# Seven products instead of eight for each pair of chunks in two down projections

## The reference

```python
h = rms_norm(x, ffn_norm_g[l])                       # first block
g = jnp.einsum('bld,df->blf', h, w_gate[l])
u = jnp.einsum('bld,df->blf', h, w_up[l])
x = x + jnp.einsum('blf,fd->bld', jax.nn.silu(g) * u, w_down[l])
...
n2 = rms_norm_2(h, norm_mlp_pre[l])                  # second block
hid = jnp.square(jax.nn.relu(jnp.einsum('bsd,df->bsf', n2, w_up[l])))
mlp_out = jnp.einsum('bsf,fd->bsd', hid, w_down[l])
h = h + rms_norm_2(mlp_out, norm_mlp_post[l])
```

## Time and profile before

| | |
|---|---|
| median of three runs | 758.38 us |
| the profiled execution | 758.59 us |
| its span, first to last instruction | 757.3 us (1.3 us less) |
| TensorE clock granted | 0.999 of full speed |
| PE matmul busy | 739.8 us, 98% |
| PE weight load busy | 641.1 us, 85% |
| DVE busy | 457.8 us, 60% |
| ACT busy | 373.3 us, 49% |
| POOL busy | 112.5 us, 15% |
| DMA | 130.46 MB, mean 172 GB/s |

### The profile page before, as it was taken

One profiled execution on the slowest core, in us unless ns is written; L12 is line 12 of the kernel. 1 busy time (PEld: TensorE's weight loads), 2 busy tenths in 40 slices (PEclk: granted clock), 3 DMA queues, 4 the chain that ended last, 5 costly groups with the idle time before them and its releaser, 6 DMA issues.

```text
span 757.3 us, 11043 instructions
## 1 busy us (share of the span) xinstructions
PE 739.8 (98%) x4394; PEld 641.1 (85%) x4394; DVE 457.8 (60%) x635; ACT 373.3 (49%) x535; POOL 112.5 (15%) x138
## 2 busy tenths in 40 slices
PE   6999999999999999999999999999999999999996
PEld 5877778999999999888888888888779899998895
DVE  5898695766555555465747555674948754455433
ACT  6666754644444434285443534664338644444431
POOL 2867550100000000001110000000302111001110
PEclk9999999999999999999999999999999999999999
DMA  9642142787665666446536543474535766656511
GB/s 318 207 132 82 58 160 92 229 284 220 189 212 172 195 216 208 133 142 219 169 110 195 194 139 112 123 250 147 178 107 198 260 192 187 206 184 191 180 46 56
DMA packets 70179, 130.46 MB, mean 172 GB/s; under 512 B 5312, under 2 KB 29072, under 8 KB 70128
## 3 DMA queue, kind: packets, MB, share of 16 engines
q1 hardware_dynamic: 68144, 125.00, 52.3%
q0 software_dynamic: 1552, 4.20, 1.7%
q10 hardware_dynamic: 432, 0.56, 0.2%
HBM read 128.62 MB, written 1.05 MB: 171 GB/s over the span
## 4 chain that ended last, share of the span: by engine, by line
PE 93%; DVE 3%; DMA 2%; issue 1%; ACT 1%; SPq 0%; DVEq 0%; ACTq 0%
PE psum L453 41%; PE psum L888 29%; PE psum L506 12%; PE psum L930 2%; DMA w_raw<-in_w_in 2%; PE psum L680 1%; PE psum L601 1%; PE psum L546 1%; PE psum L631 1%; PE psum L1058 1%; PE psum L582 1%; PE psum L652 1%; DVE b_ratio L2154 0%; PE psum L992 0%; PE psum L1020 0%
## 5 line engine op out<-in xcount | busy, mean ns | idle before, releaser
L1908 DVE TENSOR_TENSOR w_lo<-w_raw,w_hi 128x1024 fp32r<-128x1024 f32 x225 | 275.2, 1235 | 158.3 <-ACT w_hi L1284 157.7
L1284 ACT ACTIVATE w_hi<-w_raw 128x1024 fp32r<-128x1024 f32 x231 | 241.2, 1059 | 180.7 <-PE psum L888 78.6
L888 PE MATMUL psum<-h_hi,w_hi 128*128 128x256 f32 x608 | 170.3, 284 | 0.6 <-issue 0.6
L888 PE MATMUL psum<-h_hi,w_lo 128*128 128x256 f32 x608 | 169.5, 283 | 0.0
L888 PE MATMUL psum<-h_lo,w_hi 128*128 128x256 f32 x608 | 161.8, 281 | 0.0
L888 PEld LDWEIGHTS psum<-h_hi,w_hi 128*128 128x128 f32 x608 | 114.7, 189 | 1.7 <-issue 0.7
L888 PEld LDWEIGHTS psum<-h_hi,w_lo 128*128 128x128 f32 x608 | 114.4, 188 | 0.0
L888 PEld LDWEIGHTS psum<-h_lo,w_hi 128*128 128x128 f32 x608 | 111.1, 189 | 0.7
L453 PE MATMUL psum<-w_hi,h_hi 128*128 128x512 f32 (+1 forms) x240 | 94.5, 394 | 0.0
L453 PE MATMUL psum<-w_hi,h_lo 128*128 128x512 f32 (+1 forms) x240 | 93.0, 387 | 0.0
L453 PE MATMUL psum<-w_lo,h_hi 128*128 128x512 f32 (+1 forms) x240 | 92.9, 387 | 0.0
(11 more groups left out here) (303 smaller groups left out, 992.7 us busy)
## 6 DMA issues: line engine op xcount, KB each, us to landing
w_raw<-in_w_in SPq DMA_DIRECT2D x77, 512.0 KB, 4.5
w_raw<-in_w_down SPq DMA_DIRECT2D x54, 512.0 KB, 4.3
w_raw<-in_w_up SPq DMA_DIRECT2D x32, 512.0 KB, 4.4
w_raw<-in_w_gate SPq DMA_DIRECT2D x44, 256.0 KB, 2.9
w_raw<-in_w_up SPq DMA_DIRECT2D x44, 256.0 KB, 3.4
w_raw<-in_w_out SPq DMA_DIRECT2D x16, 512.0 KB, 4.0
w_raw<-in_w_branch_a SPq DMA_DIRECT2D x4, 512.0 KB, 4.6
w_raw<-in_w_branch_b SPq DMA_DIRECT2D x4, 512.0 KB, 4.6
```

The source lines that it names most:

```text
L888: mm = pe.matmul(outs, x[:, cols], y[:, kc, :], start=kc == 0 and n == 0, stop=kc == KC - 1 and n == (1 if i == 0 else 2))
L1284: act.activation(T.w_hi[:, k % SLOTS, :], T.w_raw[:, k % RAW_SLOTS, :], ACT.Copy).then_inc(S.w_rounded, 1)
L1908: dve.tensor_tensor(T.w_lo[:, k % SLOTS, :], T.w_raw[:, k % RAW_SLOTS, :], T.w_hi[:, k % SLOTS, :], ALU.subtract).then_inc(S.w_cut, 1)
```

## The change

The chunks of a down projection are taken in pairs (11 in the first, 16 in the second). The pair's product is a 2 x 2 block product: hidden values in four quarters (2 chunks x 2 token tiles), weights in four quarters (2 chunks x 2 output halves). Except in the last pair of each block it is formed with seven products of sums of quarters, where there were eight plain ones (Winograd's form of Strassen's method). `PRODUCT` gives each product's hidden quantity, weight quantity and PSUM bank; each is three matmuls of 512 columns.

- **Weight quarters.** POOL's queue brings them: `load_pair` the first three (768 KB), `load_twice` the fourth, written twice (512 KB), and `add_pair`, which adds the first two quarters, read from where they landed in SBUF, onto the two copies (an accumulating DMA, 512 KB, SBUF to SBUF). DVE forms two more sums (`sum_pair`, `sum_pair_rest`). ACT rounds and DVE cuts seven quantities, in parts of 3, 2 and 2 (`round_pair`, `cut_pair`). The arrays are laid out on the host so that each partition's data are contiguous.
- **Hidden quarters.** ACT first copies the up product out of PSUM (`take_up`, `take_hidden`). DVE forms four more quantities (`sum_hidden`, `_2`, `_3`), seven of 128 columns are rounded and cut. The second block's squares move from POOL to ACT.
- **PSUM.** The seven products hold banks 0 to 6 through the whole block; up has bank 7 alone, so each two up chunks wait until ACT has copied the two before.
- **Slots.** In the feed-forward parts fills have four slots; the other four hold every second pair's seven quantities.
- **End of a block.** The last but one pair ends products 1, 6, 7 and 5, from which ACT and DVE form what is added to each output quarter; the last pair is computed plainly into the banks of products 4, 2 and 3 and into bank 7 (`down_quarters`).

The diff, cut to its core:

```diff
+PRODUCT = {1: (1, 0, 2), 2: (3, 2, 0), 3: (7, 1, 5), 4: (2, 6, 6), 5: (5, 3, 1), 6: (6, 5, 3), 7: (4, 4, 4)}
+EARLY, LATE, MIXED, OWN = (1, 2, 3), (7, 5, 6, 4), (1, 6, 7, 5), (4, 2, 3)
+NEEDS = {1: 1, 2: 1, 3: 1, 7: 2, 5: 2, 6: 3, 4: 3}
+QUARTERS = {1: ((0, 0, 6), (1, 0, 0), (1, 1, 5), (0, 1, 7)), 2: ((0, 0, 6), (0, 1, 7), (1, 0, 0), (1, 1, 5))}
...
+    def down(q, products, first=False, last=False):
+        buf, i = pair_place(q)
+        pe.wait_ge(S.hidden_cut, q + 1)
+        for n_product, p in enumerate(products):
+            x, y, b = PRODUCT[p]
+            pe.wait_ge(S.pair_cut, pair_parts(q) + NEEDS[p])
+            x_hi, x_lo = T.hid_hi[:, i, x - 1, :], T.hid_lo[:, i, x - 1, :]
+            y_hi, y_lo = T.pair_hi[buf][:, y, :], T.pair_lo[buf][:, y, :]
+            for n, (u, v) in enumerate(((x_hi, y_hi), (x_hi, y_lo), (x_lo, y_hi))):
+                mm = pe.matmul(bank[b][:], u, v, start=first and n == 0, stop=last and n == 2)
...
+    up_first("up1", CUT["h2"], NORM["h2"], True, turn_x_right)
+    up_two(W.first["up1", 2], 3)
+    pe.wait_ge(S.up_taken, 2)
+    up_two(W.first["up1", 3], 7)
+    up_two(W.first["up1", 4], 6)
+    for i in range(2, PAIRS1):
...
+            pe.wait_ge(S.up_taken, 2 * i)
+            up_two(W.first["up1", 2 * i], 7)
+        down(i - 2, EARLY, first=i == 2)
+        pe.wait_ge(S.up_taken, 4 if i == 2 else 2 * i + 1)
+        up_two(W.first["up1", 2 * i + 1], 7)
...
+        down(i - 2, LATE, first=i == 2)
+    down(LAST1 - 1, MIXED, last=True)
+    down(LAST1 - 1, OWN)
+    down_quarters(1, QUARTERS[1][:3])
+    turn_pairs(T.x, (0, 1), (4, 6), [[(S.x_added, 9)], [(S.x_added, 10)]])
+    down_quarters(1, QUARTERS[1][3:])
...
+    pe.wait_ge(S.mixed_read, 1)
     product_piece("z", 1, 0)
+    turn_pairs(T.x, (2, 3), (2, 3), [[(S.x_added, 12)], ()])
     product_piece("z", 1, 1)
...
+    up_first("up2", CUT["h4"], NORM["h4"], False)
+    up_two(W.first["up2", 4], 3)
+    for i in range(2, PAIRS2):
+        if i > 2:
+            pe.wait_ge(S.up_taken, 2 * PAIRS1 + i)
+            up_two(W.first["up2", 2 * i], 7)
...
+        down(FIRST2 + i - 2, EARLY, first=i == 2)
...
+        down(FIRST2 + i - 2, LATE, first=i == 2)
+    down(LAST2 - 1, MIXED, last=True)
+    down(LAST2 - 1, OWN)
+    down_quarters(2, QUARTERS[2])
...
+            round_pair(q, 0)
+            round_hidden(q)
+            round_pair(q, 1)
+            if k < len(W.fills):
+                round_fill(k)
+            round_pair(q, 2)
+            if i > 2:
+                take_hidden(i)
+                square_hidden(i)
+            if k < len(W.fills):
+                round_fill(k + 1)
...
+            sum_hidden(q, 2 * PAIRS1 + i)
+            sum_hidden_2(q)
+            sum_hidden_3(q)
+            cut_pair(q, 0)
+            sum_pair(q)
+            cut_hidden(q)
+            sum_pair_rest(q)
+            cut_pair(q, 1)
+            if k < len(W.fills):
+                cut_fill(k)
+            cut_pair(q, 2)
+            if k < len(W.fills):
+                cut_fill(k + 1)
...
     post_out(0)
     add_out2(0)
-    cut_fill(W.first["up2", 0] + 0)
+    cut_fill(W.first["up2", 0] + 2)
     post_out(1)
     add_out2(1)
...
+    def load_twice(q):
...
+        elif q not in (1, FIRST2 + 1):
+            pool.wait_ge(S.pair_cut, pair_parts(q - 2) + 2)
+        pool.dma_start(T.pair_t[:, i, 0:n, :], W.pairs[q][:, 3:4, :].broadcast_to([P, n, WIDE])).then_inc(S.twice_landed[i], 16)
+    def load_pair(q):
...
+        elif q not in (0, FIRST2):
+            pool.wait_ge(S.pair_cut, pair_parts(q - 1))
+        pool.dma_start(T.pair_raw[i], W.pairs[q][:, 0:3, :]).then_inc(S.pair_landed[i], 16)
+    def add_pair(q):
+        i = pair_place(q)[1]
+        pool.wait_ge(S.twice_landed[i], pair_loads(q))
+        pool.wait_ge(S.pair_landed[i], pair_loads(q))
+        pool.dma_start(T.pair_t[:, i], T.pair_raw[i][:, 0:2, :], accum_op=ALU.add).then_inc(S.pair_added[i], 16)
...
+    pool.wait_ge(S.w_used, W.first["o", 1])
+    load_twice(FIRST2)
+    load_pair(FIRST2)
+    load_twice(FIRST2 + 1)
+    add_pair(FIRST2)
     for t in range(TILES):
         pool.wait_ge(S.post_mean, t + 1)
         root(T.stat[:, 4 + 2 * t:5 + 2 * t]).then_inc(S.post_root, 1)
     pool.wait_ge(S.x_mean, 4)
     root(T.row_scale[:, 3, :]).then_inc(S.x_root, 1)
+    load_pair(FIRST2 + 1)
+    add_pair(FIRST2 + 1)
+    for q in range(FIRST2 + 2, LAST2 + 1):
+        load_twice(q)
+        load_pair(q)
+        if q < LAST2:
+            add_pair(q)
```

More of the change, by code:

```diff
@@ L198, in used @@
     def used(self, name):
[L200 to L201 removed]
+        return self.first[name] + {"kva": 2}.get(name, 4)
 SEMAPHORES = """
@@ new lines, in up_two @@
+    def up_two(k, b):
+        for j in range(2):
+            up_group(k + j, bank[b][:, j * SEQ:(j + 1) * SEQ])
+    def down(q, products, first=False, last=False):
[8 more added lines that the diff above has]
+                mm = pe.matmul(bank[b][:], u, v, start=first and n == 0, stop=last and n == 2)
+            if last:
+                mm.then_inc(S.product_done, 1)
+        if products == LATE:
+            mm.then_inc(S.pair_used, 1)
@@ new lines, in down_quarters @@
+    def down_quarters(block, some):
+        q = (LAST1, LAST2)[block - 1]
+        buf, i = pair_place(q)
+        pe.wait_ge(S.hidden_cut, q + 1)
+        pe.wait_ge(S.pair_cut, pair_parts(q) + 2)
+        for t, half, b in some:
+            if b == 7:
+                pe.wait_ge(S.up_taken, 2 * PAIRS1 if block == 1 else 2 * PAIRS1 + PAIRS2)
+            for c in range(2):
+                y = ((0, 3), (2, 1))[c][half]
+                x_hi, x_lo = T.hid_hi[:, i, 2 * c + t, :], T.hid_lo[:, i, 2 * c + t, :]
+                y_hi, y_lo = T.pair_hi[buf][:, y, :], T.pair_lo[buf][:, y, :]
+                for n, (u, v) in enumerate(((x_hi, y_hi), (x_hi, y_lo), (x_lo, y_hi))):
+                    mm = pe.matmul(bank[b][:], u, v, start=b == 7 and c == 0 and n == 0, stop=c == 1 and n == 2)
+            mm.then_inc(S.quarter_done, 1)
@@ new lines, in copy_first @@
+    def copy_first(block):
+        act.wait_ge(S.pair_cut, pair_parts((LAST1, LAST2)[block - 1]))
+        act.wait_ge(S.product_done, len(MIXED) * (block - 1) + 1)
+        act.activation(T.form[block][0], bank[2][:], ACT.Copy).then_inc(S.first_copied, 1)
+    f = W.first["up1", 0]
+    round_to(f + 6)
+    take_up(0)
+    take_up(1)
+    round_fill(f + 6)
+    silu(0)
+    round_fill(f + 7)
+    silu(1)
+    for i in range(1, PAIRS1):
+        round_pair(i - 1, 0)
+        take_up(2 * i)
+        round_fill(f + 4 * i + 4)
+        silu(2 * i)
+        round_fill(f + 4 * i + 5)
+        round_hidden(i - 1)
+        round_pair(i - 1, 1)
+        round_pair(i - 1, 2)
+        take_up(2 * i + 1)
+        round_fill(f + 4 * i + 6)
+        silu(2 * i + 1)
+        if i < LAST1:
+            round_fill(f + 4 * i + 7)
@@ L1886, in scalar_program @@
+    copy_first(2)
+    for n, (t, half, _) in enumerate(QUARTERS[2]):
+        square_last(n, t, half, T.last[t, half])
     act.wait_ge(S.x_posted, 8)
@@ new lines, in vector_program, with end_last, scale_last @@
+    scale = [T.row_scale[:, 3, t:t + 1] for t in range(TILES)]
+    def end_last(n):
+        t, half, b = QUARTERS[2][n]
+        dve.wait_ge(S.quarter_done, 4 + n + 1)
+        own()
+        dve.tensor_tensor(T.last[t, half], bank[b][:], T.last[t, half], ALU.add).then_inc(S.formed, 1)
+    def scale_last(n):
+        t, half, _ = QUARTERS[2][n]
+        cols = slice(half * WIDE, (half + 1) * WIDE)
+        dve.wait_ge(S.formed, n + 1)
+        u = dve.scalar_tensor_tensor(T.tmp[:, t, cols], T.last[t, half], scale[t], T.bg[1][:, cols], ALU.mult, ALU.mult)
+        if half == 1:
+            u.then_inc(S.post_scaled, 1)
```

650 lines of the change are left out of this document (420 added, 230 removed).

## The result

The changed kernel took **783.27 us** (median of 4 runs, 778.5 to 784.06), the kernel before on the same chip 758.61 (4 runs, 758.03 to 759.13): ratio **1.031**, 95% interval 1.0289 to 1.0331. Forecast were 752.3 us and a range of 746 to 763. The forecast was wrong in sign, and the time lies outside its range. One execution of experiment 3 (770.64 us) is left aside for its lower mean granted clock, 0.91 where its other execution had 0.987.

A forecast was written before the change was run, and what follows sets the result against it. PE, busy 98% of the span, was taken as the bound. Span: 757.3 - 17.5 - 0.5 + 2.0 + 4.1 + 1.9 + 3.6 + 0.2 = 751.1 us; with 1.3 outside 752.4, stated as 752.3, 8-in-10 range 746 to 763.

The forecast's parts named there:

- some 7.5 us from the first issue, 7.0 from its own: Landing time of a pair's 768 KB load with 512 KB ahead of it in its queue.
- the circle of the second block: Load 7.0, sum 5.5, DVE and issue 7.0: 19.5 us against 21.2 over two steps; PE waits if transfers exceed 14.2.
- if the transfers of POOL land in the middle of its other work: One of three conditions under which the prediction said it would be wrong; no size given.
- Rival 2 (slow sums): Adding transfers take 9.1 us, PE waits each second-block step, 768 us; decides from 7.8 us on; chance 0.14.
- Entry of the second block: Second feed-forward starts +4.1 us later because POOL waits for the first two loads before its roots.
- Third step of the second block: PE waits +1.9 us in the second feed-forward's third step because the second pair's sum lands late.
- rival 3: DVE ends last in the second block, steps of 11.3 us, 9 us more, 761 us; chance 0.08.
- First block: Start to the 144 matmuls behind the first block, forecast to take 5.5 us less.
- the pitch of the down products: Down matmuls follow each other every 0.234 us; 75 fewer save 17.5 us.
- the end of the first block: PE waits +2.0 us while DVE runs twelve instructions instead of four before the first `h3` cut.
- the tail: After PE's last product, +3.6 us: 9.4 instead of 5.8 us, as DVE is behind.
- DVE not the bound of the steady steps: In second-block steps of 10.6 us DVE is the fullest engine, 88%, but still not last.

The follow-up runs named there:

- experiment 3: Changed kernel with the adding transfers moving only 8 of each 512 columns, most of the addition left out; the profiled execution took 758.28 us.
- experiment 5: Changed kernel with PE repeating two up groups three times more in the second feed-forward's fourth step, giving loads a 17 us start once; 785.89 us.
- experiment 11: Changed kernel with GpSimd's two roots before the first sum and only the doubled quarters' loads issued by SyncE; 762.79 us.
- experiment 2: Changed kernel with the loads of pairs and doubled quarters issued by SyncE instead of GpSimd; 766.2 us.
- experiment 4: Changed kernel with pair and doubled-quarter loads issued by SyncE and GpSimd's two roots before the second feed-forward's first sum; 757.7 us.
- experiment 1: Changed kernel with GpSimd taking its two roots before the first adding transfer of the second feed-forward; 775.17 us.
- experiment 9: The kernel of experiment 4 with the pair's load split into 512 and 256 KB and DVE's third cut ahead of the fill; 749.82 us.
- experiment 6: The kernel of experiment 4 with adding transfers moving only 8 of each 512 columns; 747.92 us.

## Why the prediction was wrong

- **The step that failed: "some 7.5 us from the first issue, 7.0 from its own", the load's landing in the circle of the second block.** The term counted only the doubled quarter ahead of the load. But both the sum of the pair before and the doubled quarter stand ahead of it in the same software queue. Late, directly behind both, it measures 10.7 to 11.1 us; on time, 2.6 us behind the sum, 10.1 (experiment 5). With the sum alone ahead it measures 9.0 (experiment 11), with the doubled quarter and a sum of next to nothing 7.8 to 9.4 (3), with nothing 6.4 (5), and in the changed kernel itself 4.8 (the load of 580.60). The prediction's own way of adding would have shown that the margin was gone: 3.0 to 4.3 us and 1.84 MB at 326 GB/s, 5.6, are 7.3 to 8.6 us behind the load's own issue, and with a sum of 6.3 that is 13.6 to 14.9, around the 14.2 that the prediction itself named as the point from which PE waits in each step. It would not have shown the 10.9. With a load of 10 us or more and a sum of 6.3 the two are over 16 us together.
- **The circle that I didn't draw.** Once late, the tighter one is over one step: GpSimd's list holds the issue of load q+1 behind its wait for load q. 10.8 + 1.9 = 12.7 us, against 10.6. Measured: eleven steps from 603.57 to 742.75, 12.65 each. 11 x 2.05 = 22.6 of the 25.8 us by which this block missed its forecast; the rest lies outside these steps. That this circle is the cause is shown by breaking it: without the loads in GpSimd's list and queue the same bytes take 15 us less (experiment 2). I had listed "if the transfers of POOL land in the middle of its other work" as a way to be wrong; they held up the next transfer.
- **Rival 2 (slow sums)** had the right kind of end, and not its cause: in the changed kernel the sums take 6.3, under its 7.8. It came true in experiment 4, where the loads had left GpSimd's queue and the sums in the chain took 8.3 to 10.6 beside them: 11.4 us a step.
- **The Trainium skill** (DMA: Bandwidth & Descriptors, Issuing engines are not separate DMA queues) says that issuing from several engines saves only the sequencer's time. By that, moving the loads to SyncE would have been worth at most the 1.3 us of issues a step, and the landings would have stayed. The runs disagree: with the same bytes the landing of 768 KB fell from 11.1 to 7.4 and 7.7 us (experiment 2). Whether SyncE's queue is also the faster of the two for a load by itself was not measured apart from what stands ahead in each.
- **Entry of the second block: +4.1 forecast, +7.4 measured.** The mechanism was right: experiment 1 takes back 7.0 of the 7.4 us. What was mis-sized is the same term, the landing. The forecast's times are those of the kernel before, and the changed kernel is 2.7 us ahead of it here; so 2.7 us are to be added to its rows. GpSimd issues the first of the three transfers at 557.37 (by that count 560.1, forecast 559.5) and the sum at 566.53, 9.2 us later, where I had said 7.5. The second tile's addition starts at 572.05 (574.8, forecast 572.2).

```profile
558.09 0.55 POOL L3333 DMA_DIRECT2D pair_raw<-in_down  x1
...
566.53 0.91 POOL L3340 DMA_DIRECT2D pair_sums<-pair_raw  x1 [7.18 <-DMA pair_raw<-in_down]
```

- **The clock at that entry** was no term of the forecast. PE was idle for 4.8 us before the first tile's transposes and for 2.0 us before the second's, and over 569 to 577 us it was granted 0.50 of its clock, the level of 1.2 GHz (third figure from the right in the row). The second tile's 8 transposes took 1.97 us, 1.3 before the change, and the first 144 matmuls of the block 18.25; without the wait (experiment 9, clock 1.00) they take 17.5.

```profile
569.00:577.00 8.00, 5.98 (x28) 5.58 (x29) 6.83 (x12) 4.50 (x11) 0.55 (x1) 0.50 0.40 105
```

- **Third step of the second block: +1.9 forecast, for a sum that lands late.** The wait for ACT's copy is there in each kernel of this study and always about as long: 2.5 us in the changed kernel, 2.6 with experiment 6's small sum, 2.7 in experiment 9. So the sum isn't its cause. Ahead of it DVE is busy 13.30 of 13.40 us (585.5 to 598.9 us, experiment 9). The 48 matmuls behind the wait take 7.48 us there instead of 5.69, at a granted clock of 0.62 over their first 4 us. That is some 4.5 us instead of 1.9. DVE ends last there, which the forecast had only as rival 3.
- **First block: -5.5 forecast, -2.7 measured.** Two misses of opposite sign. The step is 16.23 us instead of 16.4, some 1.5 us in nine steps (an estimate); experiment 9, which has no stall at the start, gains 7.0 us here. Against it the changed kernel loses 4.3 us: the first pair's load took 8.79 us and its sum 8.37, both above the 7.0 and 5.5 that I had taken, and the sum landed at 157.9 us instead of 154.2. The loss isn't the same in each execution: with the same code up to here, experiment 5 comes to the 144 matmuls at 328.07 instead of 331.18.

```profile
140.19 8.79 DMA pair_raw<-in_down
149.55 8.37 DMA pair_sums<-pair_raw
...
160.82 4.63 PE psum L964 x24
```

- **Right:** the pitch of the down products (21 in 4.78 to 4.89 us are 0.228 to 0.233 each); the end of the first block (DVE's twelve instructions stand in the chain from 310.45 to 318.77, and PE goes on at 320.74, 14.9 us behind the last LATE group, where the forecast had the first `h3` cut at 14.8); the tail, 9.2 us against 9.4, of 5.8 before; DVE not the bound of the steady steps.
- **Sum check.** In experiment 9, where load and sum are short enough for the circle (6.7 to 6.9 and 6.0 to 6.5 us, but with the load split, the cut earlier and SyncE as issuer), the terms are -7.0, +0.2, -6.8 and +3.4 = -10.2 us of span, 747.1. The forecast without its entry term was -10.3. That the two agree to 0.1 us is luck: the first block gains 1.5 us more than forecast, and the second 1.6 us less.

## What to carry to other kernels

For each transfer on a loop's path, write down everything that stands ahead of it in its queue at the moment of its issue in the steady state, not only what the same iteration adds; then draw each circle, also the one through the issuing engine's own list, where a wait for transfer q stands ahead of the issue of transfer q+1. Here plain loads did not belong in the list and queue of the engine that also issues the accumulating transfers and waits for them: taking them out was worth 17 us by itself. And where a loop is a circle of transfers, a smaller first transfer or one cut done earlier shortens it with the same bytes; here each was worth 4 to 5 us.
